# The first layer's heads between the dense products of a two-layer trunk

## What is computed

```
q_lat, kv_lat, k_rope, rq, rk, rv, rg = _split(h @ w_in, (384, 256, 32, 512, 512, 1024, 1024))
qh  = (_rmsnorm(q_lat, q_norm) @ w_uq)      # 8 heads of 64 + 32 (the 32 are rotated)
kvh = (_rmsnorm(kv_lat, kv_norm) @ w_ukv)   # 8 heads of 64 keys + 64 values
mla = _causal_softmax_attention(q, k, v)    # 8 heads
ret = _retention(_rope(rq), _rope(rk), rv)  # 8 heads, scores times a decay, no softmax
ret = silu(rg) * _head_groupnorm(ret, ret_gn)
out = concat([mla, ret]) @ w_out            # 1536 x 1024, added to h
```

## Time and profile before

| what | us |
|---|---|
| median of three executions (1629.96 to 1630.76) | 1630.28 |
| the profiled execution: device time | 1629.9 |
| its span, first to last instruction | 1628.0 |
| layer 0: in-projection, from the first to after the last matmul | 14.2 to 97.8 |
| layer 0: heads | 97.8 to 173.0 |
| layer 0: out-projection | 173.0 to 208.6 |
| from there to the first matmul of the FFN | 208.6 to 219.1 |

### The profile page before, as it was taken

The page is one execution under the profiler, slowest core; times in us unless marked ns, Lnnn a source line. Parts: engine busy times, 40 slices in busy tenths (PEclk is TensorE's granted clock), DMA queues, the critical chain, the costliest instruction groups (busy, mean ns, idle before and its releaser), DMA issues.

```text
span 1628.0 us, 22810 instructions
## 1 busy us (share of the span) xinstructions
PE 1566.4 (96%) x7762; PEld 1309.8 (80%) x7762; DVE 1235.8 (76%) x1438; ACT 1086.2 (67%) x1304; POOL 25.9 (2%) x21
## 2 busy tenths in 40 slices
PE   7989989999999998999999999999999999999995
PEld 6867779999977677788888888888888888888884
DVE  4455545444556645899999999999999999999995
ACT  5444454444455553788888888888788878878874
POOL 0000000000000000000000000000000000000000
PEclk9997899999999998999999999999999999999998
DMA  9640355555643426899999999999999999999950
GB/s 330 191 153 1 104 181 182 181 182 186 214 162 108 168 104 245 313 385 367 380 387 355 391 387 345 399 388 345 400 384 350 397 384 350 399 381 353 404 213 28
DMA packets 193158, 454.86 MB, mean 279 GB/s; under 512 B 8144, under 2 KB 18256, under 8 KB 192848
## 3 DMA queue, kind: packets, MB, share of 16 engines
q1 hardware_dynamic: 190272, 443.69, 74.3%
q0 software_dynamic: 2832, 10.49, 2.5%
HBM read 447.33 MB, written 6.82 MB: 279 GB/s over the span
## 4 chain that ended last, share of the span: by engine, by line
PE 94%; DVE 3%; ACT 1%; issue 1%; DMA 0%; DVEq 0%; ACTq 0%; SPq 0%
PE bank L270 28%; PE bank L272 28%; PE bank L271 28%; PE bank L1778 2%; PE bank L1227 1%; PE bank L825 0%; PE bank L1220 0%; PE bank L832 0%; PE bank L423 0%; PE bank L1213 0%; PE bank L1212 0%; PE bank L1564 0%; PE bank L1557 0%; DMA h<-x_dram 0%; PE bank L1242 0%
## 5 line engine op out<-in xcount | busy, mean ns | idle before, releaser
L283 DVE TENSOR_TENSOR w_lo<-ring,w_hi 128x1024 fp32r<-128x1024 f32 (+1 forms) x834 | 1006.5, 1220 | 262.2 <-ACT w_hi L279 215.1
L279 ACT ACTIVATE w_hi<-ring 128x1024 fp32r<-128x1024 f32 (+1 forms) x834 | 880.4, 1059 | 359.5 <-PE bank L272 359.0
L270 PE MATMUL bank<-w_hi,xe_hi 128*128 128x512 f32 x896 | 354.3, 395 | 3.5 <-DVE w_lo L283 2.1
L272 PE MATMUL bank<-w_hi,xe_lo 128*128 128x512 f32 x896 | 350.3, 391 | 0.0
L271 PE MATMUL bank<-w_lo,xe_hi 128*128 128x512 f32 x896 | 349.6, 390 | 0.0
L270 PEld LDWEIGHTS bank<-w_hi,xe_hi 128*128 128x128 f32 x896 | 168.7, 188 | 37.6 <-DVE w_lo L283 2.2
L272 PEld LDWEIGHTS bank<-w_hi,xe_lo 128*128 128x128 f32 x896 | 168.6, 188 | 36.1
L271 PEld LDWEIGHTS bank<-w_lo,xe_hi 128*128 128x128 f32 x896 | 168.7, 188 | 34.1
L270 PE MATMUL bank<-w_hi,hT_hi 128*128 128x512 f32 x448 | 177.5, 396 | 0.0
L272 PE MATMUL bank<-w_hi,hT_lo 128*128 128x512 f32 x448 | 176.0, 393 | 0.0
L271 PE MATMUL bank<-w_lo,hT_hi 128*128 128x512 f32 x448 | 175.7, 392 | 0.0
(11 more groups left out here) (273 smaller groups left out, 1511.1 us busy)
## 6 DMA issues: line engine op xcount, KB each, us to landing
ring<-m_gate_dram SPq DMA_DIRECT2D x112, 1024.0 KB, 5.6
ring<-m_up_dram SPq DMA_DIRECT2D x112, 1024.0 KB, 6.2
ring<-m_down_dram SPq DMA_DIRECT2D x112, 1024.0 KB, 6.2
ring<-ab_w_in_dram SPq DMA_DIRECT2D x16, 936.0 KB, 6.1
ring<-f_gate_dram SPq DMA_DIRECT2D x14, 1024.0 KB, 5.1
ring<-f_up_dram SPq DMA_DIRECT2D x14, 1024.0 KB, 5.0
ring<-f_down_dram SPq DMA_DIRECT2D x14, 1024.0 KB, 4.9
ring<-cd_w_in_dram SPq DMA_DIRECT2D x11, 1024.0 KB, 5.0
```

The costliest lines, as they stand in the source:

```text
L270: nc.tensor.matmul(out_, a_hi, b_hi, start=first, stop=False, **kw)
L272: return nc.tensor.matmul(out_, a_lo, b_hi, start=False, stop=last, **kw)
L279: nc.scalar.activation(w_hi[:, buf, 0:width], src, ACT.Copy).then_inc(hi_ready, 1)
L283: nc.vector.tensor_tensor(w_lo[:, buf, 0:width], src, f32(w_hi[:, buf, 0:width]), ALU.subtract).then_inc(split_ready, 1)
```

## The change

`InProj`, `Softmax`, `mix_pe`, `mix_act` and `mix_dve` go. The 44 units of in- and out-projection of layer 0 become one loop over `d` on each engine, as in layer 1, with the heads' steps behind units. The in-projection is taken in the order and by the borders of `AB_CHUNKS` (keys' latent first, then queries' latent, retention's q and k, v, gates), one column block of 288, 384 or 512 at a time, 4 units each. The out-projection goes by row blocks: the softmax heads' 4 blocks first. Softmax values are computed transposed (`heads_out`), with the weights normalised before (`normalised`). Silu is applied as the gates leave the banks. Buffers are placed anew.

```diff
+        AB_CHUNKS = ((A_KV, 288), (0, 384), (A_RQK, 512), (A_RQK + 512, 512), (A_RV, 512), (A_RV + 512, 512),
+                     (A_RG, 512), (A_RG + 512, 512))
+        L0_UNITS = AB_UNITS + KM
+        OUT_SLOTS, OUT_LOADED = (6, 0, 1, 2, 3, 6), (2, 5, 5, 5, 5, 3)
+        MLA_S, MLA_PT, MLA_V, RT_BANK = 4, 5, 6, 7
+        R_BANK = (7, 7, 7, 6, 7, 6, 7, 6)
+        RET_AT = {24: (0,), 25: (1,), 26: (2, 3), 27: (4, 5), 28: (6, 7)}
+        RET_V_AT = {26: (0,), 27: (1, 2), 28: (3,), 29: (4, 5), 30: (6, 7)}
+        RT_AT = {16: 0, 18: 1, 20: 2, 22: 3}
...
+        def mla_at(d, lag):
+            i = d - 16 - lag
+            return i if 0 <= i < MLA_H else None
...
+            for d in range(L0_UNITS):
+                if d < AB_UNITS:
+                    project(d)
+                else:
+                    output(d)
+                if d == 4:
+                    turn_latent(lat_kv, 2, (4,), 0)
+                if d in (6, 7):
+                    keys_values(d - 6)
+                if d == 8:
+                    pe.wait_ge(kvh_done, 1)
+                    turn_latent(lat_q, 3, (5, 6), 1)
+                if d in (10, 11):
+                    queries(d - 10)
...
+                if d in RT_AT:
+                    turn_ret(RT_AT[d])
+                if mla_at(d, 0) is not None:
+                    scores(mla_at(d, 0))
+                if mla_at(d, 2) is not None:
+                    values(mla_at(d, 2))
+                if mla_at(d, 1) is not None:
+                    if d == 17:
+                        pe.wait_ge(qT_done, 2)
+                    turn(mla_at(d, 1))
+                for i in RET_AT.get(d, ()):
+                    ret_scores(i)
+                for i in RET_V_AT.get(d, ()):
+                    ret_values(i)
+                if d in (32, 35):
+                    turn_mix((d - 32) // 3)
```

That loop is TensorE's. VectorE's, in the same manner:

```diff
+            for d in range(L0_UNITS):
+                if mla_at(d, 1) is not None:
+                    minimum(mla_at(d, 1))
+                if d in (20, 22, 24, 26):
+                    mixed_lo((d - 20) // 2)
+                for i in RET_AT.get(d - 1, ()):
+                    decayed(i)
...
+                if d + 3 < L0_UNITS:
+                    l0_lo(dve, d + 3)
...
+                if d in (14, 15):
+                    rope_ret(0, d - 14)
+                if d in (17, 18):
+                    rope_ret(1, d - 17)
+                if mla_at(d, 1) is not None:
+                    normalised(mla_at(d, 1))
+                if d in (29, 31):
+                    statistics((d - 29) // 2)
+                if d in (30, 33):
+                    centred((d - 30) // 3)
+                if d in (31, 34):
+                    gated((d - 31) // 3)
+                if d in (33, 36):
+                    for k in range(4):
+                        mixed_lo(4 + k + 4 * ((d - 33) // 3))
```

And a part of ScalarE's:

```diff
+                if d + 3 < L0_UNITS:
+                    l0_hi(act, d + 3)
...
+                if mla_at(d, 1) is not None:
+                    exponentials(mla_at(d, 1))
+                if d in (30, 33):
+                    deviations((d - 30) // 3)
+                if d in (26, 31):
+                    nc.scalar.preload_act_table(ACT.Silu)
```

More of the change, by code:

```diff
@@ L38 @@
 CAP = 128
-IN_CH = 8
+AB_UNITS = 32
 UNIT = 1024
@@ L125, in trunk @@
[L125 to L131, removed]
@@ L284, in lo_unit @@
                                     ALU.subtract).then_inc(split_ready, 1)
[L287 to L374, removed]
@@ L799, in l0_dve @@
-            between = {0: [lambda: statistics(range(4, 6))], 1: [lambda: statistics(range(6, 8))],
-                       2: [lambda: variances(range(4, 8), True)],
-                       4: [lambda: normalised(0), lambda: normalised(4)], 5: [lambda: gated(0)],
-                       6: [lambda: normalised(8), lambda: normalised(12)],
-                       7: [lambda: gated(1), lambda: mla_quad(0)]}
-            for i in range(MLA_H):
-                mla.dve_step(dve, i)
-                for part in between.get(i, []):
-                    part()
@@ new lines, in queries @@
+            def queries(tb):
+                pe.wait_ge(latT_done, 2)
+                pe.wait_ge(kvh_done, 2)
+                for nh in range(2):
+                    pe.wait_ge(slot_full[4 + nh], 16)
+                    for k in range(3):
+                        ins = nc.tensor.matmul(pb[((7, 4), (5, 6))[tb][nh]][:, 0:384], latT[:, k, tb * P:tb * P + P],
+                                               ring[4 + nh][:, k * 384:k * 384 + 384], start=k == 0, stop=k == 2)
+                ins.then_inc(qkv_banked, 1)
@@ new lines, in scores, with turn @@
+            def scores(i):
+                if i:
+                    pe.wait_ge(nm_done, i)
+                q, k, s = qT[0:MLA_D, i, :], kT[0:MLA_D, i, :], pb[MLA_S]
+                nc.tensor.matmul(s[:, 0:P], q[:, 0:P], k[:, 0:P], start=True, stop=True)
+                nc.tensor.matmul(s[:, P:384], q[:, P:256], k[:, 0:256], start=True, stop=True).then_inc(s_banked, 1)
+            def turn(i):
+                pe.wait_ge(mla_p, i + 1)
+                if i:
+                    pe.wait_ge(pT_done, i)
+                for b in range(3):
+                    ins = nc.tensor.transpose(pb[MLA_PT][:, b * P:b * P + P], p_sb[i % 2][:, b * P:b * P + P],
+                                              const("ident"))
+                ins.then_inc(pT_banked, 1)
@@ L1961, in _ @@
             sp.dma_start(h, x[0].rearrange("(b p) d -> p b d", p=P)).then_inc(x_in, 16)
-            for jj in range(2):
+            for c in range(2):
                 for half in range(2):
-                    ab.load(sp, 0, jj, half)
+                    ab_load(sp, c, half)
             sp.dma_start(cst[:, FIRST_CONST:NCONST], consts[:, FIRST_CONST:NCONST]).then_inc(tables_in, 16)
+            sp.dma_start(ring[6].rearrange("p (k n) -> p k n", k=2),
+                         w_ukv[0].rearrange("(k p) n -> p k n", p=P)).then_inc(slot_full[6], 16)
             for nh in range(2):
```

813 lines of the change are left out of this document (399 added, 414 removed).

## The result

The changed kernel takes 1602.26 us in the median of four executions (1601.14 to 1602.96), the kernel before 1630.22: a ratio of 0.983, 95% interval 0.9818 to 0.9842. That is 28.0 us less where 21.8 were forecast.

A forecast was written before the change was run, and what follows sets the result against it. Layer 0's heads were taken as bound by TensorE's waits and half-speed clock. Work 53.9 - 77.2 = -23.3, waits +3.2, gains -0.4 and -1.3 give -21.8: 1629.9 to 1608.1, median 1608.5 us; range 1604 to 1617.

The forecast's parts named there:

- What bounds and what goes: Layer 0's heads: TensorE at clock 0.54 in the softmax part; 75.25 us without dense matmuls and 1.94 us in out-projection go.
- Waits: TensorE's added waits at units 17, 18, 24, 32 and 35 of layer 0, together 3.2 us.
- The upper bound of 9 for the waits: Layer 0's added waits: about 9 us if each of eight softmax steps waits as long as that of unit 18.
- What comes back, as TensorE's time at full clock: Layer 0's projections 14.9, transposes 9.4, softmax 15.6 and retention 12.9 us return between dense units, sum 52.8.
- Retention: scores 0.84, values 0.77, times eight, 12.9: Layer 0's retention heads on TensorE: each of eight priced at one head's scores and values, 12.9 us in all.
- The two small gains: Smaller first unit shortens VectorE's first split, -0.4 us; no square root table load before the FFN's norm, -1.3 us.
- The rule weighed: Skill's rule that cycling through banks with small gaps slows the clock: 1650 us by it, 1608.5 by the rows.
- The clock dips once: Waits at units 17 and 18 drop the clock for one or two units, 2.6 us each; 1611 to 1614; chance 0.16.
- VectorE or ScalarE becomes the bound: Softmax and retention steps each wait about 1 us; 1614, up to 1618 with the tail; chance 0.14.
- Slower: TensorE runs units 16 to 30 at the slow clock, 42 us more, 1650; chance 0.03.
- no effect: Whole kernel: gain and waits cancel within 0.2%; chance 0.01.
- No waits: Layer 0's steps: hand-overs are covered, so no wait is added; -25.0 us, 1605.3; chance 0.12.

The follow-up runs named there:

- Experiment 5: Against the changed kernel: the eight softmax heads taken out from between units 16 to 25 and done in one piece behind unit 23; 1611.58 us.
- Experiment 1: Against the changed kernel: VectorE's rotation of retention's second part, at units 17 and 18, moved behind the normalising of the softmax weights; 1598.97 us.
- Experiments 2 and 4: Two runs against the changed kernel: retention's paired heads taken from the same row half, 1604.43 us; retention heads 0 and 1 made a pair, 1600.86 us.
- experiment 3: Against the changed kernel: Silu's table loaded at unit 36, so the square root's table is loaded again before the FFN's norm; 1603.44 us.

## Why the prediction was right and where it failed

**What bounds and what goes: right.** The stretch of 75.25 us is gone, the clock stays at 1.00 from 20 to 180 us, and TensorE is the engine that sets the end of each step but for three waits. Experiment 5 shows what the dense units between the softmax steps are worth: without them 10.1 of the 28 us are lost. The other 18 come with the rest of the change (projections, transposes and retention between units, values computed transposed), and no run takes these apart. One reading of mine was wrong: TensorE did not wait "a little in each step" of the old softmax heads. Half of the eight steps show no wait, and the clock stayed down all the same.

**Waits: right in cause, the sum by luck.** Unit 17: 1.6 forecast, 1.83 measured. Unit 18: 0.6 and 0.91. Unit 35: 0.5 and 0.47. Units 24 and 32: 0.3 and 0.2, none measured. The sum is 3.2 either way, but only because the first two are 0.5 too small and the last two 0.5 too large. Experiment 1 shows the cause of the first two. The upper bound of 9 for the waits doesn't follow from its own words: eight times the 0.6 of unit 18 and the others are 5.8. No load released ScalarE in the first 40 us, and between 13.97 and 81.03 TensorE waits for nothing.

**"What comes back, as TensorE's time at full clock": the failing step.** Its 52.8 us were mis-sized, by the table above, each named term in the same direction; only the switches went the other way.
- "Retention: scores 0.84, values 0.77, times eight, 12.9" took 9.6. For the scores, -2.4, the price of one head alone was multiplied by eight although six of the heads were to stand in pairs. Experiments 2 and 4 show that the overlap comes from the different row halves: 0.86 against 1.50 for a pair, 1.9 us for three. The diff shows the pairs (`RET_AT`), and the trace before had the price of one. For the values, -0.9, I took the distance up to a matmul of another kind; two heads in a row take 1.25 (138.37 to 139.62), so 0.63 each.
- "Ten take 1.25, eight take 1.04, so 0.13 each": I took the length of the group where its cost is the distance to the next start, 0.79 for eight. I had stated that very rule for dense matmuls. (74 times 0.13 would be 9.6 at that, not 9.4.)
- "Softmax 8 by 1.95": 1.84. The second score matmul starts 0.22 behind the first, where in layer 1 it took 0.33.
- The projections' 14.9 held the length of the last matmul and the switches ahead and behind; by starts they are 13.2. "0.04 for the switches" was too small, as the last row of the table shows. These two nearly cancel.

**The two small gains**: -1.3 for the table load was exact in the wait, 7.02 before and 5.74 after; experiment 3 has 2.0 in the medians. The first split gave its 0.4: from VectorE's start on it to the first matmul are 0.80 us (13.17 to 13.97) instead of 1.18 (13.02 to 14.20). VectorE itself started 0.15 later, which leaves the 0.23; in the eleven traces of kernels with these first units the first dense matmul lies anywhere from 13.74 to 14.39.

**The rule weighed.** TensorE cycles through the heads' banks 4 to 7 behind each unit and keeps clock 1.00, so the trace disagrees here with the rule of the Trainium skill ("TensorE: Matmul & The Clock Gate", "A second HAM failure mode: psum-queue depth-cycling") as I read it. The gaps between groups on which that section rests its rule hardly occur here: 3.2 us of idle time in 160. The rows were the better guide.

**The rivals.** *The clock dips once* did not happen: a wait of 1.83 us inside the units left the window from 80 to 100 us at 1.00. *VectorE or ScalarE becomes the bound* did not: from unit 19 on no step waits for either, up to the 0.47 us of unit 35. *Slower* and *no effect* did not come either. *No waits* at 1605.3 is the nearest in time and wrong in its reason. The range failed with its lower end, because it varied only the waits and took every price of TensorE's work as known; an error common to all the cases moved them together.

## What to carry to other kernels

Price work that moves from one place to another by the distance between starts, and look in the trace for the same instructions in the neighbourhood that they will have: alone, in a row, in a pair. Where heads of 64 rows or 64 columns meet, set those of different halves next to each other; then see whether the time that this frees was covering another engine's chain. And on an engine that works in order, put what others wait for ahead of what nobody waits for: here that was one exchange of lines for 2.5 us.

## What the hardware showed that I had not expected

- Float32 matmuls on different halves of the array ran side by side without anything being asked for: rows, 0.86 us for two heads' scores against 1.50 in the same half; columns, 0.81 for two heads' values, as long as one head's (91.00 to 91.79). The Trainium skill, "TensorEngine Tiling (Array Packing)", section "Tiling Modes", says that tiles operate independently and that changing the mode drains the engine; the first agrees with the traces. Of a drain no run here takes the cost apart: a unit next to a step is 0.1 to 0.3 us longer than one without (2.84 to 2.99 against 2.73), and other costs of the switch lie in that as well.
- Behind the idle time before the FFN TensorE runs at half pace for 3.3 to 5.8 us, and how long does not follow from the length of the wait: 5.6 us behind a wait of 5.73 in one execution, 3.9 behind 7.02 in another.
- The clock at the start varied between executions of kernels whose first units are the same: half pace up to 17.96 us in one and up to 20.31 in another, worth about 1 us. The granted clock of the window from 13 to 25 us reads 1.00 and 0.72; so a window can read 1.00 although four of its microseconds ran at half pace.
